# Projections of a two-layer decoder step: split single-pass products replaced by plain float32 products

## The chip, the cores and the metric

The kernel runs on one core of one Trainium2 chip. The metric is the device time of one execution in microseconds (us). TensorE is called PE in the profile and its weight loads PEld, VectorE DVE, ScalarE ACT, GpSimd POOL, and SyncE, which here orders nearly all transfers, SP (its queue SPq).

## The reference

One step of a decoder with two layers, all in float32: a retention layer, a shared key and value projection, and a block-sparse attention layer. 320 tokens pass through every projection: 256 of a prompt and 64 of eight sample sequences. The width is 1024.

```python
def retention_layer(x, pos, S0, chunk, norm_w, w_in, gn_w, w_out):
    h = rmsnorm(x, norm_w) @ w_in                  # 1024 -> q 1024 | k 1024 | v 2048 | gate 2048
    q, k, v, g = jnp.split(h, ...)
    q, k = rotary(q), rotary(k) * RET_DK ** -0.5
    S_fin, o = lax.scan(retention_chunk, S0, (q, k, v))
    y = (rmsnorm(o, gn_w) * silu(g)) @ w_out       # 2048 -> 1024
    return x + y, S_fin

def shared_kv(x, kv_norm_w, w_kv, k_norm_w):
    k, v = jnp.split(rmsnorm(x, kv_norm_w) @ w_kv, 2)   # 1024 -> 2048
    return rmsnorm(k, k_norm_w), v

def moba_query(x, norm_w, w_in, q_norm_w):
    q, g = jnp.split(rmsnorm(x, norm_w) @ w_in, 2)      # 1024 -> 2048
    ...
# attention over the own block and the past block, then * silu(g), @ moba_w_out (1024 -> 1024), + x
```

## The kernel before

The weights of all projections are cut into 52 chunks of 1 MB (`make_schedule`, `chunk_source`): `rq`, `rk`, `rv`, `rg` of each of four retention heads, `ro`, then `mq`, `mk`, `mv`, `mg`, `mo`. A chunk is loaded by SP into one of `RAW` = 3 slots of `w_raw`, two chunks ahead. One list of steps, written by hand in `make_schedule`, is walked by every engine, and each takes its own part of each step; a step `MM` is a piece of a projection (`project`), and the steps of the attention and retention work are put in the gaps between such pieces.

The projections are made with single-pass products (type fp32r). Each float32 operand is held as a rounded part and a remainder. For the weights, ACT writes the rounded part `w_hi` (`split_hi`, recorded at line 1246) and DVE the remainder `w_lo` (`split_lo`, line 1584), a quarter of a chunk at a time (steps `WS`), two chunks in turn. For the tokens they are `xn_hi`, `xn_lo` and `ym_hi`, `ym_lo`. A product is then three matmuls, hi·hi + hi·lo + lo·hi.

There are three kinds of step on PE, each for 128 rows of the inner dimension ("a k-step"):

- Line 944: 32 chunks (`rq`, `rk`, `rg`, `ro`, `mq`, `mg`), 128 weight columns as the stationary operand, 320 token columns moving. 32 chunks x 2 tiles x 8 = 512 k-steps, three matmuls each.
- Line 941: 20 paired chunks (`rv`, `mk`, `mv`, `mo`), 128 prompt tokens stationary, 512 weight columns moving. 20 x 2 tiles x 4 = 160 k-steps, three matmuls each.
- Line 925: the 64 sample tokens in the same 20 chunks. Their rounded parts and remainders stand side by side as 128 stationary columns (`stacked`), so a k-step is two matmuls, with `w_hi` and with `w_lo` moving: 80 k-steps. The upper 64 rows of the result are added to the lower ones afterwards (`lower_half`, `upper_half`).

Other products of the kernel that the prediction reads: the scores (line 1006), the states against the queries on four column tiles of 32 (line 1059), a sum over squares (line 1082) and the transposes (line 996); lines 1006, 1059 and 1082 are plain float32. In the program, a `matmul` of line 1082 stands once for each head, four in all.

Of the kernel before, what the change touches and what calls it, by code (L numbers as in the profile page):

```python
# [34 lines left out]
P = 128  # L35
D = 1024
# [12 lines left out]
RAW = 3  # L49
# [99 lines left out]
def make_schedule():  # L149
# [9 lines left out]
    def chunk(kind, a, b, gaps):  # L159
# [4 lines left out]
        starts = {0: 0} if n == 3 else {0: 0, 1: 2}  # L164
        mids = {0: 1, 1: 2, 2: 3} if n == 3 else {0: 1, 1: 3}
        size = KT // 2 if paired else KT
        whole = c + 1 if paired and b == 0 else c
        for pos, i in enumerate(tile_order(kind, a, b)):
            if pos in starts:
                steps.append(("WS", c + 1, starts[pos]))  # L170
# [10 lines left out]
            if pos in mids:  # L181
                steps.append(("WS", c + 1, mids[pos]))
# [131 lines left out]
def build(nc, a):  # L314
# [3 lines left out]
    with ctx:  # L318
# [113 lines left out]
        yf = flat_ktc[:, :, 2 * (TP + P):D]  # L432
# [11 lines left out]
        yfs = wide.ap().rearrange("p n k -> p (n k)")[:, 0:4 * P].rearrange("p (h i) -> p h i", h=MH)  # L444
# [22 lines left out]
        w_hi_done, w_lo_done, first_lo_done = sem("w_hi_done"), sem("w_lo_done"), sem("first_lo_done")  # L467
# [6 lines left out]
        unsplit_done = sem("unsplit_done")  # L474
        x_hi_done, x_lo_done = sem("x_hi_done"), sem("x_lo_done")
# [13 lines left out]
        y_done, y_hi_done, y_lo_done = sem("y_done"), sem("y_hi_done"), sem("y_lo_done")  # L489
# [21 lines left out]
        stack_done = sem("stack_done")  # L511
        q_done, gate_done, tanh_done = sem("q_done"), sem("gate_done"), sem("tanh_done")
        yf_done, yfs_done = sem("yf_done"), sem("yfs_done")
# [26 lines left out]

        def await_lo(eng, c, n):

            if c == 0 and n == 3:
                eng.wait_ge(first_lo_done, 1)
            else:
                eng.wait_ge(w_lo_done, 4 * c + n if c else (2, 1, 3)[n])
# [39 lines left out]
        hi_parts = [s for s in steps if s[0] in ("YA", "PG")]  # L586
        lo_parts = [s for s in steps if s[0] in ("YB", "PG")]

        def y_hi(*step):

            return 3 * KT + hi_parts.index(step) + 1

        def y_lo(*step):

            return 3 * KT + lo_parts.index(step) + 1

        def await_ret_over(eng):
# [4 lines left out]
            eng.wait_ge(y_lo_done, RH)  # L602
# [10 lines left out]
        def y_parts(h):  # L613

            k0 = 4 * (h % 2)
            hi, lo = (ym_hi, ym_lo) if h < 2 else (xn_hi, xn_lo)
            return hi[:, k0:k0 + 4, 0:T], lo[:, k0:k0 + 4, :]
# [50 lines left out]
        def _(sp):  # L668
# [197 lines left out]
        def _(pe):  # L866
# [18 lines left out]
            def project(step):  # L885
# [14 lines left out]
                hi, lo = chunk_view(w_hi, c, c % 2), chunk_view(w_lo, c, c % 2)  # L900
                x_hi, x_lo = xn_hi[:, :, 0:T], xn_lo
                if kind in ("mq", "mg") or (kind, h) == ("ro", 0):
                    x_hi, x_lo = ym_hi, ym_lo
                first = {"mq": 16, "mk": 24}.get(kind) if h == 0 and i == 0 else None
                stacked = paired and i == 2
                if stacked and h == 0 and k0 == 0:
                    pe.wait_ge(stack_done, {"rv": 1, "mk": 2, "mv": 2, "mo": 3 + part}[kind])
                for pos in range(k0, k1):
                    wk = FIRST_K[pos] if c == 0 else pos
                    k = base + wk  # L910
                    if c == 0:
# [3 lines left out]
                        pe.wait_ge(w_hi_done, pos // 2 + 1)  # L915
                        pe.wait_ge(x_hi_done, pos + 1)
                    elif i == tile_order(*chunks[c])[0] and paired:
                        await_lo(pe, c, wk)
                    elif i == 0 and not paired and k % 2 == 0:
                        await_lo(pe, c, k // 2)  # L920
                    if kind == "ro" and part == 0 and i == 0 and k % 4 == 0:
                        pe.wait_ge(y_lo_done, 2 * h + k // 4 + 1)
# [5 lines left out]
                    if first:  # L928
                        pe.wait_ge(x_lo_done, first - 8 + k + 1)
                    if kind == "mo" and h == 0 and i == 0:  # L930
                        pe.wait_ge(x_lo_done, y_lo("YB", k))
                    terms = ((hi, x_hi), (hi, x_lo), (lo, x_hi)) if c else ((hi, x_hi), (lo, x_hi), (hi, x_lo))
                    for n, (w, x) in enumerate(terms):
                        flags = {"start": base + pos == 0 and n == 0, "stop": k == KT - 1 and n == 2}
                        if c == 0 and n == 1:
                            await_lo(pe, c, k // 2)
                        elif c == 0 and n == 2:
                            pe.wait_ge(x_lo_done, pos + 1)
                        if paired:
                            c0, m = TOK[i]  # L940
                            mm = pe.matmul(bank[b][0:m, :], x[:, k, c0:c0 + m], w[:, wk, :], **flags)  # L941
                            continue
                        for tile, out in tiles:
                            mm = pe.matmul(bank[out][:, 0:T], w[:, wk, P * tile:P * tile + P], x[:, k, :], **flags)  # L944
                            if flags["stop"]:
                                close(mm, out)
# [281 lines left out]
        def _(act):  # L1228
# [6 lines left out]
            def split_hi(c, n):  # L1235

                if c >= nchunks:
                    return
                if c == 0 and n < 2:
                    act.wait_ge((second_w_loaded, first_w_loaded)[n], 16)  # L1240
                elif n == (2 if c == 0 else 0):
                    act.wait_ge(w_loaded[c % RAW], 16 * (c // RAW + 1))
                    if c >= 2:
                        await_chunk_used(act, c - 2)
                part = slice(CW // 4 * n, CW // 4 * (n + 1))
                act.activation(w_hi[:, c % 2, part], w_raw[:, c % RAW, part], ACT.Copy).then_inc(w_hi_done, 1)  # L1246

# [8 lines left out]
            for step in steps:  # L1256
                kind = step[0]
                if kind == "WS":
                    split_hi(*step[1:])
                elif kind == "XC" and step[2] == 1:  # L1260
                    await_full(act, 5, "UR", step[1])
                    act.activation(cross[:, :], bank[5][:, :], ACT.Copy).then_inc(bank_read[5], 1)
                elif kind == "W":
                    kt = step[1]
                    await_read(act, *tile_use("ro", KT + kt))
                    if kt == 0:
                        await_read(act, 3, "RP")
                        await_full(act, *tile_use("ro", KT - 1))
                    act.activation(ym_hi[:, kt, :], xT[:, kt, :], ACT.Copy, scale=wcols[:, W_MOBA + kt:W_MOBA + kt + 1])\
                        .then_inc(x_hi_done, 1)  # L1270
                elif kind == "SQ":
                    kt = step[1]
                    await_read(act, *tile_use("ro", KT + kt))
                    if kt == 0:
                        act.wait_ge(y_lo_done, RH)
# [5 lines left out]
                elif kind == "NB":  # L1281
                    kt = step[1]
                    if kt == KT:
                        continue
                    if kt == 0:
                        await_full(act, *tile_use("ro", 2 * KT - 1))
                    act.wait_ge(unsplit_done, kt + 1)
                    act.activation(xn_hi[:, kt, 0:T], scr[:, kt, :], ACT.Copy).then_inc(x_hi_done, 1)
                elif kind == "ST":
                    n = step[1]  # L1290
                    act.wait_ge(x_lo_done, (8, 24, y_lo("PG", 0), y_lo("PG", 1))[n])
                    if n:
                        await_full(act, *tile_use(*(("rv", 11), ("mv", 5), ("mv", 5))[n - 1]))
                    ks_at = slice(0, KT) if n < 2 else slice(4 * n - 8, 4 * n - 4)
                    if n == 0:
                        act.wait_ge(sums_done, 2)
                        act.activation(rms[:, 0:2], rms[:, 0:2], ACT.Sqrt, bias=eps[:, 0:1], scale=1.0 / D).then_inc(roots_done, 1)
                        act.activation(rms[0:TS, 2:3], rms[0:TS, 2:3], ACT.Sqrt, bias=eps[0:TS, 0:1], scale=1.0 / D)\
                            .then_inc(roots_done, 1)
# [805 lines left out]
```

## Time and profile before

| what | value |
|---|---|
| median of 3 runs | 501.36 us (498.37 to 502.27) |
| profiled execution | 499.55 us, its span 497.5 us |
| granted TensorE clock | 1.00 |
| PE busy | 490.3 us, 99% of the span |
| DVE, ACT, POOL busy | 353.1, 259.5, 95.9 us |
| transfers | 125.56 MB, mean 252 GB/s |

PE's busy time is the union of its instructions, whose ends are modelled: neighbours overlap, and the mean duration of one (317 ns) is longer than the distance from one start to the next. What a matmul occupies is read from the distance of the starts, or from the chain of work that ended last, where a run of matmuls is put down with its length and count.

### The profile page before, as it was taken

The numbers are of one execution on the slowest core, as the hardware profiler recorded it, in microseconds if no ns is written. First come the engines' busy times: TensorE is split into PE (matmuls) and PEld (weight loads), VectorE is DVE, ScalarE is ACT, GpSimd is POOL, SyncE is SP. The second block draws the span as 40 slices with busy tenths as digits, with TensorE's granted clock in tenths as the row PEclk, the third lists the DMA queues.
The fourth block names the chain that finished last, engine by engine and source line by source line (L and its number), as shares of the span: only waits on it lengthen the run. The fifth ranks groups of instructions, "written<-read, shape, count | busy, mean of one in ns | idle before, by whom it ended". The sixth has DMA issues, their size and how long they took to land.

```text
span 497.5 us, 9935 instructions
## 1 busy us (share of the span) xinstructions
PE 490.3 (99%) x3713; PEld 425.2 (85%) x3713; DVE 353.1 (71%) x629; ACT 259.5 (52%) x533; POOL 95.9 (19%) x139
## 2 busy tenths in 40 slices
PE   8999999999999999999999999999999999999997
PEld 7789978899778997799799999986777788999885
DVE  3875629895598838897189988897976764776631
ACT  5826533366416734385363454773747655555430
POOL 0192003620063200910000033437002000000000
PEclk9999999999999999999999999999999999999999
DMA  8984887999899998999946998999769666683211
GB/s 251 358 303 155 244 301 255 366 370 263 242 333 394 282 218 307 343 374 235 231 155 211 327 334 203 274 237 213 208 230 328 234 235 231 234 308 117 86 53 54
DMA packets 86915, 125.56 MB, mean 252 GB/s; under 512 B 5507, under 2 KB 51796, under 8 KB 86740
## 3 DMA queue, kind: packets, MB, share of 16 engines
q1 hardware_dynamic: 86018, 124.63, 80.8%
q8 instruction: 30, 0.49, 0.4%
q0 software_dynamic: 768, 0.28, 0.4%
q14 instruction: 17, 0.14, 0.1%
q10 hardware_dynamic: 82, 0.02, 0.0%
HBM read 98.93 MB, written 27.57 MB: 254 GB/s over the span
## 4 chain that ended last, share of the span: by engine, by line
PE 91%; DMA 3%; ACT 2%; DVE 1%; SPq 1%; issue 1%; DVEq 0%
PE bank L944 44%; PE bank L941 20%; PE bank L925 7%; DMA w_raw<-in_ret_w_in 3%; PE bank L1059 3%; PE bank L1121 2%; PE bank L1183 2%; PE bank L1073 1%; PE bank L1006 1%; PE bank L1222 1%; PE bank L1039 1%; PE bank L1041 1%; PE bank L1040 1%; PE bank L1027 1%; PE bank L1209 1%
## 5 line engine op out<-in xcount | busy, mean ns | idle before, releaser
L1584 DVE TENSOR_TENSOR w_lo<-w_raw,w_hi 128x512 fp32r<-128x512 f32 x207 | 145.2, 740 | 70.0 <-ACT w_hi L1246 69.3
L1246 ACT ACTIVATE w_hi<-w_raw 128x512 fp32r<-128x512 f32 x208 | 118.9, 620 | 70.2 <-PE bank L944 35.4
L944 PE MATMUL bank<-xn_hi,w_hi 128*128 128x320 f32 x320 | 100.0, 317 | 0.2 <-DVE raw_qk L1674 0.2
L944 PE MATMUL bank<-xn_hi,w_lo 128*128 128x320 f32 x320 | 97.7, 309 | 0.0
L944 PE MATMUL bank<-xn_lo,w_hi 128*128 128x320 f32 x320 | 97.5, 309 | 0.0
L941 PE MATMUL bank<-w_hi,xn_hi 128*128 128x512 f32 x160 | 65.1, 407 | 0.0
L944 PEld LDWEIGHTS bank<-xn_hi,w_hi 128*128 128x128 f32 x320 | 59.7, 188 | 3.9 <-issue 2.3
L941 PE MATMUL bank<-w_lo,xn_hi 128*128 128x512 f32 x160 | 62.6, 391 | 0.0
L941 PE MATMUL bank<-w_hi,xn_lo 128*128 128x512 f32 x160 | 62.4, 390 | 0.0
L944 PE MATMUL bank<-ym_hi,w_hi 128*128 128x320 f32 x192 | 60.9, 317 | 0.0
L944 PEld LDWEIGHTS bank<-xn_lo,w_hi 128*128 128x128 f32 x320 | 59.8, 188 | 0.3
L944 PEld LDWEIGHTS bank<-xn_hi,w_lo 128*128 128x128 f32 x320 | 59.7, 188 | 0.2 <-POOL w_lo L1985 0.2
L944 PE MATMUL bank<-ym_hi,w_lo 128*128 128x320 f32 x192 | 59.3, 309 | 0.0
L944 PE MATMUL bank<-ym_lo,w_hi 128*128 128x320 f32 x192 | 59.3, 309 | 0.0
L1798 DVE SCALAR_TENSOR_TENSOR st<-st,bank 128x512 f32<-128x512 f32 x64 | 39.6, 681 | 5.1 <-PE bank L1073 5.1
L944 PEld LDWEIGHTS bank<-ym_hi,w_hi 128*128 128x128 f32 x192 | 36.1, 188 | 1.8 <-issue 1.7
L2007 POOL TENSOR_TENSOR fin<-raw_qk,cst 128x320 f32<-128x320 f32 x16 | 16.9, 1076 | 106.1 <-DMA out_ret_state_prompt<-fin 96.8
L941 PEld LDWEIGHTS bank<-w_hi,xn_hi 128*128 128x128 f32 x160 | 30.0, 188 | 8.5 <-issue 3.1
L944 PEld LDWEIGHTS bank<-ym_lo,w_hi 128*128 128x128 f32 x192 | 36.1, 188 | 0.1
L944 PEld LDWEIGHTS bank<-ym_hi,w_lo 128*128 128x128 f32 x192 | 36.0, 188 | 0.0
L941 PEld LDWEIGHTS bank<-w_lo,xn_hi 128*128 128x128 f32 x160 | 30.0, 188 | 6.7
L941 PEld LDWEIGHTS bank<-w_hi,xn_lo 128*128 128x128 f32 x160 | 30.1, 188 | 5.5
(291 smaller groups left out, 777.1 us busy)
## 6 DMA issues: line engine op xcount, KB each, us to landing
w_raw<-in_ret_w_in SPq DMA_DIRECT2D x23, 1024.0 KB, 11.2
st<-in_state_ret SPq DMA_DIRECT2D x32, 512.0 KB, 8.7
out_ret_state_sample<-st SPq DMA_DIRECT2D x32, 512.0 KB, 3.8
w_raw<-in_ret_w_out SPq DMA_DIRECT2D x8, 1024.0 KB, 9.0
w_raw<-in_moba_w_in SPq DMA_DIRECT2D x8, 1024.0 KB, 6.3
w_raw<-in_w_kv SPq DMA_DIRECT2D x8, 1024.0 KB, 8.2
cache<-in_cache_v SPq DMA_DIRECT2D x16, 512.0 KB, 4.4
cache<-in_cache_k SPq DMA_DIRECT2D x44, 128.0 KB, 4.5
```

Of the source, the lines that this page charges most:

```text
L925: mm = pe.matmul(bank[b][:, :], xn_hi[:, k, TP:T + TS], w[:, wk, :], start=k == 0 and n == 0, stop=k == KT - 1 and n == 1)
L941: mm = pe.matmul(bank[b][0:m, :], x[:, k, c0:c0 + m], w[:, wk, :], **flags)
L944: mm = pe.matmul(bank[out][:, 0:T], w[:, wk, P * tile:P * tile + P], x[:, k, :], **flags)
L1006: mm = pe.matmul(bank[5][0:m, col:col + n], kT[:, d, j:j + m], qT[:, d, i0:i0 + n], start=d == 0, stop=d == 1)
L1027: mm = pe.matmul(o[:, P:TP], vp[:, 1, at], sT_own[:, :], start=False, stop=True)
L1059: mm = pe.matmul(bank[5][32 * j:32 * j + 32, :], qz[:, q0:q0 + 32], st[:, b, DV * d:DV * d + DV], start=False, stop=g == 1 and d == 1, ski ...
L1121: last[g] = pe.matmul(bank[PS_BANKS[g]][c0:c0 + 32, 0:PAST], wide[rows_at, 8 * h + 2 * e + q // 2, at:at + 32], turned(q, s)[rows_at, :, 4 ...
L1183: mm = pe.matmul(bank[7][32 * j:32 * j + 32, P * u:P * u + P], window(8 * half_at + 4 * (j // 2) + 2 * pg + j % 2, b % 4), page_at(16 + m) ...
L1246: act.activation(w_hi[:, c % 2, part], w_raw[:, c % RAW, part], ACT.Copy).then_inc(w_hi_done, 1)
L1584: dve.tensor_tensor(w_lo[:, c % 2, part], w_raw[:, c % RAW, part], w_hi[:, c % 2, part].bitcast(F32), ALU.subtract).then_inc(w_lo_done, 1)
L1798: dve.scalar_tensor_tensor(state, state, math.exp(NEW * LOG_DECAY[h]), bank[up_bank(b, d)][:, :], ALU.mult, ALU.add).then_inc(bank_read[up ...
L2007: done(pool.tensor_tensor(to, x, tab, ALU.mult))
```

## The change

All splitting of weights and tokens is gone. `w_raw` itself is the operand, the tokens are one tensor `xn` (and `ym`), and each k-step is one plain float32 matmul. `RAW` is 7, in the space that `w_hi` and `w_lo` took; SP orders two chunks ahead at first and up to six ahead later, and a slot is free when PE has used its chunk. For the sample tokens, 64 columns are stationary; even k-steps write rows 0 to 63 of the bank and odd ones rows 64 to 127, two column tiles of the array, and the halves are added as before.

```diff
-RAW = 3
+RAW = 7
...
-        w_hi = sb("w_hi", [P, 2, CW], F32R)
-        w_lo = sb("w_lo", [P, 2, CW], F32R)
...
-        xn_hi = sb("xn_hi", [P, KT, T + TS], F32R)
-
-        xn_lo = sb("xn_lo", [P, KT, T], F32R)
-        ym_hi = sb("ym_hi", [P, KT, T], F32R)
-        ym_lo = sb("ym_lo", [P, KT, T], F32R)
+        xn = sb("xn", [P, KT, T])
+        ym = sb("ym", [P, KT, T])
...
                 if c >= RAW:
-                    await_lo(sp, c - RAW, 2)
-                    await_lo(sp, c - RAW, 3)
+                    await_chunk_used(sp, c - RAW)
...
+            ordered = 2
             for step in steps:
                 kind = step[0]
                 if kind == "CHUNK":
                     c = step[1]
-                    load_chunk(c + 2)
+                    while ordered <= c + min(RAW - 1, 2 + c // 2):
+                        load_chunk(ordered)
+                        ordered += 1
...
+                if c and k0 == 0 and i == tile_order(*chunks[c])[0]:
+                    pe.wait_ge(w_loaded[c % RAW], 16 * (c // RAW + 1))
...
                     if stacked:
-                        for n, w in enumerate((hi, lo)):
-                            mm = pe.matmul(bank[b][:, :], xn_hi[:, k, TP:T + TS], w[:, wk, :],
-                                           start=k == 0 and n == 0, stop=k == KT - 1 and n == 1)
+                        rows_at = slice(TS * (k % 2), TS * (k % 2) + TS)
+                        mm = pe.matmul(bank[b][rows_at, :], x[:, k, TP:T], w[:, wk, :], start=k < 2, stop=k >= KT - 2,
+                                       skip_group_check=True)
                         continue
...
-                    terms = ((hi, x_hi), (hi, x_lo), (lo, x_hi)) if c else ((hi, x_hi), (lo, x_hi), (hi, x_lo))
-                    for n, (w, x) in enumerate(terms):
...
-                        for tile, out in tiles:
-                            mm = pe.matmul(bank[out][:, 0:T], w[:, wk, P * tile:P * tile + P], x[:, k, :], **flags)
...
+                    if paired:
+                        c0, m = TOK[i]
+                        mm = pe.matmul(bank[b][0:m, :], x[:, k, c0:c0 + m], w[:, wk, :], **flags)
+                        continue
+                    for tile, out in tiles:
+                        mm = pe.matmul(bank[out][:, 0:T], w[:, wk, P * tile:P * tile + P], x[:, k, :], **flags)
...
-                act.activation(w_hi[:, c % 2, part], w_raw[:, c % RAW, part], ACT.Copy).then_inc(w_hi_done, 1)
...
-                dve.tensor_tensor(w_lo[:, c % 2, part], w_raw[:, c % RAW, part], w_hi[:, c % 2, part].bitcast(F32),
-                                  ALU.subtract).then_inc(w_lo_done, 1)
```

The step lists of the two kernels place the same work in the same gaps. On PE, this is the end of a prompt tile and the start of the sample tile of chunk 8, the first `rv` chunk of the second head, in the kernel before (a name such as `bank<-w_hi,xn_lo` gives the output, the moving and the stationary operand):

```order
L941 MATMUL bank<-w_hi,xn_hi 128x512
L941 MATMUL bank<-w_hi,xn_lo 128x512
L941 MATMUL bank<-w_lo,xn_hi 128x512
L925 MATMUL bank<-w_hi,xn_hi 128x512
L925 MATMUL bank<-w_lo,xn_hi 128x512
```

and this the same place and the next chunk in the changed kernel, where L904 is a prompt k-step, L898 a sample k-step, L907 one with 320 token columns, and L1036, L1040 and L1045 are the old lines 1073, 1077 and 1082:

```order
L1036 MATMUL bank<-vq,kq 128x512 x4
L904 MATMUL bank<-w_raw,xn 128x512 x4
L898 MATMUL bank<-w_raw,xn 64x512 x4
L1040 MATMUL bank<-eye,scr 128x128 x4
L904 MATMUL bank<-w_raw,xn 128x512 x8
L898 MATMUL bank<-w_raw,xn 64x512 x2
L1045 MATMUL bank<-scr,ones 128x320
L898 MATMUL bank<-w_raw,xn 64x512 x2
L907 MATMUL bank<-xn,w_raw 128x320 x8
```

The three and the two matmuls of a k-step have become one, and the sample k-steps stand in 27 unbroken runs of two or four, which have another tile shape than nearly all of their neighbours.

On SP, the loads of chunks 2 to 6 before (L683 loads a chunk, L693 a state of a sample sequence):

```order
L683 DMA w_raw<-in_ret_w_in 128x4x512 x2
L683 DMA w_raw<-in_ret_w_in 128x8x256
L693 DMA st<-in_state_ret 128x2x512 x2
L683 DMA w_raw<-in_ret_w_in 128x8x256
L753 DMA bias_line<-gs 8x392
L754 DMA pages<-in_page_table 1x16
L756 DMA eye<-in_c_eye 128x4
L693 DMA st<-in_state_ret 128x2x512 x2
L683 DMA w_raw<-in_ret_w_in 128x8x256
L693 DMA st<-in_state_ret 128x2x512 x2
```

and now (L652 and L662 are the same two):

```order
L652 DMA w_raw<-in_ret_w_in 128x4x512 x2
L652 DMA w_raw<-in_ret_w_in 128x8x256 x2
L662 DMA st<-in_state_ret 128x2x512 x2
L652 DMA w_raw<-in_ret_w_in 128x8x256
L725 DMA bias_line<-gs 8x392
L726 DMA pages<-in_page_table 1x16
L728 DMA eye<-in_c_eye 128x4
L662 DMA st<-in_state_ret 128x2x512 x2
L652 DMA w_raw<-in_ret_w_in 128x8x256
L652 DMA w_raw<-in_ret_w_in 128x4x512
L662 DMA st<-in_state_ret 128x2x512 x2
```

One chunk more is ordered ahead of the first states, and two ahead of the third pair; before the last two, SP now waits until PE has used chunks 0 and 1.

On ACT, the start of the kernel before (L1297 and L1298 the roots for the norm, L1336 the copies of `xT`):

```order
L1246 ACTIVATE w_hi<-w_raw 128x512 x2
L1297 ACTIVATE rms<-rms,eps 128x2
L1298 ACTIVATE rms<-rms,eps 64x1
L1300 ACTIVATE xn_hi<-xn_lo 128x8x64
L1246 ACTIVATE w_hi<-w_raw 128x512 x4
L1336 ACTIVATE xT<-bank 128x320 x4
```

and now:

```order
L1263 ACTIVATE xn<-bank,wcols 128x320
L1287 ACTIVATE raw_qk,rms<-st 64x512
L1231 ACTIVATE rms<-rms,eps 128x2
L1232 ACTIVATE rms<-rms,eps 64x1
L1268 ACTIVATE xT<-bank 128x320 x4
L1327 ACTIVATE vp<-bank,rms 128x512 x2
```

The copies of `xT` no longer stand behind six weight splits, the last two of which waited for chunk 2.

## Rows read from the trace of the kernel before

**Rows 1.** The page: span, busy time of TensorE, and the chain by engine.

```profile
span 497.5 us, 9935 instructions
...
PE 490.3 (99%) x3713; PEld 425.2 (85%) x3713; DVE 353.1 (71%) x629; ACT 259.5 (52%) x533; POOL 95.9 (19%) x139
...
PE 91%; DMA 3%; ACT 2%; DVE 1%; SPq 1%; issue 1%; DVEq 0%
```

**Rows 2.** Waits of TensorE: who was waited for, us, times, longest.

```profile
PE bank L964 <- POOL eps L1964: 1.7, 1, 1.7
PE bank L1086 <- ACT xT L1336: 1.0, 1, 1.0
```

**Rows 3.** Groups of TensorE by form: count | busy us, mean ns of one.

```profile
L944 PE MATMUL bank<-xn_hi,w_hi 128*128 128x320 f32 x320 | 100.0, 317 | 0.2 <-DVE raw_qk L1674 0.2
...
L941 PE MATMUL bank<-w_hi,xn_hi 128*128 128x512 f32 x160 | 65.1, 407 | 0.0
...
L925 PE MATMUL bank<-w_hi,xn_hi 128*128 128x512 f32 x80 | 33.0, 413 | 0.0
...
L1059 PE MATMUL bank<-st,qz 128*32 128x512 f32 x128 | 14.6, 595 | 0.0
...
L1082 PE MATMUL bank<-scr,ones 128*128 128x320 f32 x8 | 2.8, 432 | 0.0
...
L996 PE MATMUL bank<-eye,kT 128*128 128x128 f32 x16 | 2.4, 271 | 0.0
```

**Rows 4.** The chain in order of time: start us, us, what.

```profile
33.39 1.81 PE bank L925 x8
35.20 5.44 PE bank L941 x24
...
42.45 3.52 PE bank L944 x24
...
71.68 3.57 PE bank L1059 x32
...
99.00 0.54 PE bank L1082 x2
...
103.98 0.44 PE bank L996 x4
```

**Rows 5.** Weight loads of TensorE (PEld), same columns as Rows 3.

```profile
L944 PEld LDWEIGHTS bank<-xn_hi,w_hi 128*128 128x128 f32 x320 | 59.7, 188 | 3.9 <-issue 2.3 <-DVE raw_qk L1674 0.7 <-DVE w_lo L1584 0.2
```

**Rows 6.** Timeline of TensorE, 51.35 to 52.3 us: start, us, what.

```profile
51.18 0.65 PE L1006 MATMUL bank<-qT,kT 128*128 128x128 f32 x5
51.76 0.42 PE L944 MATMUL bank<-xn_hi,w_hi 128*128 128x320 f32 x1
52.02 0.31 PE L944 MATMUL bank<-xn_lo,w_hi 128*128 128x320 f32 x1
```

**Rows 7.** Timeline of TensorE in the first two chunks.

```profile
22.11 0.31 PE L944 MATMUL bank<-xn_hi,w_lo 128*128 128x320 f32 x1
23.37 0.60 PE L1086 MATMUL bank<-fin 32*8 32x264 f32 x2 [0.95 <-ACT xT L1336]
24.14 0.41 PE L944 MATMUL bank<-xn_hi,w_hi 128*128 128x320 f32 x1 [0.17 <-DVE raw_qk L1674]
```

**Rows 8.** The chain before 24.14 us.

```profile
10.89 10.18 DMA w_raw<-in_ret_w_in
...
21.10 0.64 ACT w_hi L1246
...
21.76 0.56 DVE w_lo L1584
```

**Rows 9.** The page, transfers: KB each, us from issue to landing.

```profile
st<-in_state_ret SPq DMA_DIRECT2D x32, 512.0 KB, 8.7
```

**Rows 10.** Waits of the sync queue, same columns as Rows 2.

```profile
SPq L546 <- DVE w_lo L1584: 63.8, 12, 9.2
SPq L539 <- DVE st L1798: 62.1, 25, 13.0
```

More of the change, by code:

```diff
@@ L584, in x_pieces, with y_count @@
             return KT // 2 if chunks[c][0] in PAIRED else KT
[L586 to L595, printed above, removed]
+        gated = [s for s in steps if s[0] in ("YA", "PG")]
+        def y_count(*step):
+            return 3 * KT + gated.index(step) + 1
         def await_ret_over(eng):
@@ L899, in project @@
                     await_free(pe, b, "TILE", whole, i)
[L900 to L903, printed above, removed]
+                w = chunk_view(w_raw, c, c % RAW)
+                x = ym if kind in ("mq", "mg") or (kind, h) == ("ro", 0) else xn
+                if c and k0 == 0 and i == tile_order(*chunks[c])[0]:
+                    pe.wait_ge(w_loaded[c % RAW], 16 * (c // RAW + 1))
                 first = {"mq": 16, "mk": 24}.get(kind) if h == 0 and i == 0 else None
                 stacked = paired and i == 2
-                if stacked and h == 0 and k0 == 0:
-                    pe.wait_ge(stack_done, {"rv": 1, "mk": 2, "mv": 2, "mo": 3 + part}[kind])
+                if stacked and kind == "mo" and h == 0 and k0 == 0:
+                    pe.wait_ge(x_done, y_count("PG", part))
                 for pos in range(k0, k1):
@@ L914, in project @@
                             turn_x(2, *TOK[2], range(4, KT))
[L915 to L920, printed above, removed]
-                    if kind == "ro" and part == 0 and i == 0 and k % 4 == 0:
-                        pe.wait_ge(y_lo_done, 2 * h + k // 4 + 1)
+                        if pos % 2 == 0 and pos < 6:
+                            pe.wait_ge((first_w_loaded, second_w_loaded, w_loaded[0])[pos // 2], 16)
@@ L923, in project @@
+                        pe.wait_ge(x_done, pos + 1)
+                    if kind == "ro" and part == 0 and i == 0 and k % 4 == 0:
+                        pe.wait_ge(y_moved, 2 * h + k // 4 + 1)
+                    if first:
+                        pe.wait_ge(x_done, first - 8 + k + 1)
+                    if kind == "mo" and h == 0 and i == 0:
+                        pe.wait_ge(x_done, y_count("YA", k))
                     if stacked:
-                        for n, w in enumerate((hi, lo)):
-                            mm = pe.matmul(bank[b][:, :], xn_hi[:, k, TP:T + TS], w[:, wk, :],
-                                           start=k == 0 and n == 0, stop=k == KT - 1 and n == 1)
+                        rows_at = slice(TS * (k % 2), TS * (k % 2) + TS)
+                        mm = pe.matmul(bank[b][rows_at, :], x[:, k, TP:T], w[:, wk, :], start=k < 2, stop=k >= KT - 2,
+                                       skip_group_check=True)
@@ new lines, in project @@
+                    flags = {"start": base + pos == 0, "stop": k == KT - 1}
+                    if paired:
[4 more added lines that the diff above has]
+                        mm = pe.matmul(bank[out][:, 0:T], w[:, wk, P * tile:P * tile + P], x[:, k, :], **flags)
+                        if flags["stop"]:
+                            close(mm, out)
@@ L1257, in _ @@
                 kind = step[0]
-                if kind == "WS":
-                    split_hi(*step[1:])
-                elif kind == "XC" and step[2] == 1:
+                if kind == "XC" and step[2] == 1:
                     await_full(act, 5, "UR", step[1])
@@ L1280, in _ @@
                         .then_inc(bank_read[5], 1)
[L1281 to L1299, printed above, removed]
-                    act.activation(xn_hi[:, ks_at, T:T + TS], xn_lo[:, ks_at, TP:T].bitcast(F32), ACT.Copy).then_inc(stack_done, 1)
+                elif kind == "ST" and step[1] == 0:
+                    act.wait_ge(sums_done, 2)
+                    act.activation(rms[:, 0:2], rms[:, 0:2], ACT.Sqrt, bias=eps[:, 0:1], scale=1.0 / D).then_inc(roots_done, 1)
+                    act.activation(rms[0:TS, 2:3], rms[0:TS, 2:3], ACT.Sqrt, bias=eps[0:TS, 0:1], scale=1.0 / D)\
+                        .then_inc(roots_done, 1)
                 elif kind == "RP":
@@ L1344, in _ @@
                     scaled(0)
-                    split_hi(0, 0)
                     scaled(1)
@@ L1494, in _ @@
                         await_full(act, *tile_use("rg", 15))
-                    act.activation(y_parts(h)[0], y_now(h), ACT.Copy).then_inc(y_hi_done, 1)
+                    act.activation(y_at(h), y_now(h), ACT.Copy).then_inc(y_moved, 1)
                 elif kind == "MB":
@@ L1625, in _ @@
                 kind = step[0]
[L1626 to L1634 removed]
+                if kind == "NORM":
                     for kt in range(2):
@@ L1683, in _ @@
                     done.wait()
-                elif kind == "NB":
+                elif kind == "NB" and step[1] < KT:
                     kt = step[1]
-                    if kt < KT:
-                        normed(kt, W_KV, xT[:, kt, :])
-                    if kt:
-                        dve.wait_ge(x_hi_done, 2 * KT + kt)
-                        dve.tensor_tensor(xn_lo[:, kt - 1, :], scr[:, kt - 1, :], xn_hi[:, kt - 1, 0:T].bitcast(F32),
-                                          ALU.subtract).then_inc(x_lo_done, 1)
+                    if kt == 0:
+                        await_full(dve, *tile_use("ro", 2 * KT - 1))
+                    dve.scalar_tensor_tensor(xn[:, kt, :], xT[:, kt, :], wcols[:, W_KV + kt:W_KV + kt + 1], rsb[:, :],
+                                             ALU.mult, ALU.mult).then_inc(x_done, 1)
                 elif kind == "MP":
@@ L1845, in _ @@
                         own_values_lo(step[1] + 1)
-                elif kind == "SH":
-                    h = step[1]
-                    dve.wait_ge(y_hi_done, h + 1)
-                    hi, lo = y_parts(h)
-                    dve.tensor_tensor(lo, y_now(h), hi.bitcast(F32), ALU.subtract)\
-                        .then_inc(y_lo_done, 1)
                 elif kind == "MB":
@@ L1968, in _ @@
             cos, sin = cst[:, C_COS:C_COS + T], cst[:, C_SIN:C_SIN + T]
-            part = slice(3 * CW // 4, CW)
             def spread_queries(h):
```

142 lines of the change are left out of this document (19 added, 123 removed).

## The prediction

> **What bounds the kernel now.** I read the page first, then the waits of TensorE, its groups by form, and the chain in order of time. The page has PE busy for 99% of the span, and 91% of the chain that ended last is PE's own work [rows 1]. The view has six waits of PE, and only two reach a microsecond: 1.7 us before anything is loaded, and 1.0 us in the second chunk [rows 2]. So no wait on the splits of ACT and DVE bounds this kernel, however busy these two are; the matmuls themselves do. What the change is worth is decided by one question: does a k-step take PE longer as one plain float32 product than as three (or two) single-pass ones?
>
> The mean durations of the groups (317 ns, 432 ns) are not what a matmul occupies, since neighbours overlap. The chain gives the distances [rows 4]. 24 single-pass matmuls of 320 columns take 3.52 us, 0.147 each; 24 of 512 columns take 5.44 us, 0.227 each; 8 of line 925 take 1.81 us, 0.226 each.
>
> **The projections before.** 512 k-steps x 3 x 0.147 = 225.8 us; 160 x 3 x 0.227 = 109.0; 80 x 2 x 0.226 = 36.2. Together 371 us of a span of 497.5.
>
> **A plain product of 320 columns.** Line 1082 is this very shape, in plain float32. It stands four times in the program and has 8 records [rows 3], so a plain product is recorded as two, and the two occupy 0.54 us of the chain [rows 4]. That is 0.27 for a record against 0.147 for a single-pass product of equal width: each record streams the columns twice. A weight load takes 188 ns [rows 5] and fits under a record of 270. A k-step goes from 0.441 to 0.54 us: 512 x 0.10 = **+51 us** (the bounds 0.535 and 0.55, the rounding of the row and some margin, give +48 to +56).
>
> **A plain product of 512 columns.** By width, 0.54 x 512 / 320 = 0.864 us. The states against the queries (line 1059) have 512 columns too, on four column tiles: 32 records in 3.57 us are eight rounds of 0.446, the entry into this shape included, or 0.89 for two rounds [rows 4]. I take 0.86, since the row includes an entry of about 0.1. The k-step was 0.681: 160 x 0.18 = **+29 us** (+28 to +33).
>
> **The sample tokens.** One product of 64 stationary columns costs its full stream, 0.86 us, but even and odd k-steps stand on different column tiles. Line 1059 shows that column tiles run beside each other: 32 records, each of 0.43 us by width, would take 13.8 us one after another and take 3.57 [rows 4]. With two tiles I take full overlap, 0.43 us for a k-step, against 0.45 before: 80 x -0.02 = **-2 us**. With no overlap at all it would be 80 x 0.41 = +33; nothing in the row reads that way.
>
> **Changing the tile shape.** These k-steps were of full width and are now 27 runs of half width between full ones. What such a change costs is seen where line 1006 goes to 64 columns and back [rows 6]. One record of 128 columns and four of 64 start at 51.18; by 0.54/640 us for a column they occupy 0.32 us, so PE would be free at 51.50, and the next matmul starts at 51.76: 0.26 us for in and out. The one after it comes 0.26 later instead of 0.147, another 0.11, because its weight load could not be made ahead; behind a record of 0.27 us it would nearly hide. 27 x 0.26 = 7.0, with a part of the 0.11 some **+8 us** (from +4, if runs next to other shapes change nothing, to +10).
>
> The Trainium skill has a rule that speaks against the change at this place: changing the tiling mode, not just the tile, drains TensorE (TensorEngine Tiling, "Key Properties"). The trace agrees with it in kind, by the 0.26 us just read, and the page gives no figure, so the sum would be the same.
>
> **What the change gives back on PE.** In the order of the program I count 86 runs of projection matmuls that follow other work. Each now loses about 0.11 us at its second matmul [rows 6], since a weight load of 188 ns is longer than a product of 147 and could not be made ahead. Behind records of 0.27 and 0.43 us it mostly hides: 86 x 0.06 = **-5 us** (0 to -9).
>
> **The start.** PE waits 0.95 us at 23.37 for ACT's copies of `xT`, in a gap of 1.26 us between starts, and once more before 24.14 [rows 7]. Behind it stand the splits of chunk 2: its load lands at 21.07, ACT splits until 21.74, DVE goes on [rows 8]. Without splits the copies of `xT` come earlier and these gaps go, **-1.7 us** (0 to -2.5). Later is then only PE itself, whose first two chunks grow by their k-steps.
>
> **What costs nothing.** The splits on ACT and DVE, four on each for each of 52 chunks, leave engines that PE almost never waits for. Where tokens are scaled, one instruction replaces two or three; no wait of PE ends there now [rows 2]. The seven slots hide loads that are hidden already: no wait of PE for a weight load is among its waits from the second chunk on. If that cover went, a load would have to come a whole chunk late, and six ahead makes it less likely.
>
> **The new wait on SP.** A slot is now free when PE has used a chunk, so at every chunk SP stands until the chunk before it is used, where it stood for the last split, 63.8 us in all [rows 10]. Behind it are queued the loads and stores of the sample states, the key pages, and the rows through memory for the next update; PE's line 1059 waits for those states. SP already keeps pace with the state updates, 62.1 us of waits for DVE's `st` [rows 10], which are in the same chunks as PE. I take 0, and a bound below.
>
> **Sum.** 51 + 29 - 2 + 8 - 5 - 1.7 = +79.3 us. The profiled execution took 499.55 us, which gives 579; the median of the runs is 1.8 above it. I predict **580 us**, a ratio of 1.157. The terms' own bounds, taken together (low ends +69, high ends +95), would make 570 to 596; not all err on one side, so I hold 572 to 590 for this case.
>
> **Rivals.**
>
> *Two column tiles overlap only in part.* A plain product is two records. If records start strictly in program order, then the two of one product stand back to back on their own tile, and only the second of one product runs beside the first of the next: four k-steps take five slots of 0.43 us instead of four, two k-steps three instead of two. That is one slot more for each run, 27 x 0.43 = +11.6: **592 us**. Against it: by the same rule the 32 records of line 1059 would be paired at best and take 6.9 us, and they take 3.57 [rows 4]. The Trainium skill says that matmuls start and end in program order and are never reordered (TensorE: Matmul & The Clock Gate, Part 3, "The mechanism"); the row of line 1059 does not go with it for products of two records, unless the build interleaves them. Chance 0.08.
>
> *No overlap of the two tiles:* +35 on the sum, **615 us**. Against it, the same row. Chance 0.03.
>
> *SP comes late.* If in each of the three heads with states to reload the last states land one landing time too late (8.7 us [rows 9]), PE stands 26 us: **606 us**. It decides once SP reaches a load later than 8.7 us before its product; a chunk will take PE 8.6 us, so the margin is about a chunk. Against it: states are loaded a whole head ahead of use. Chance 0.05.
>
> *Not slower: the projections as one record.* The transposes on line 996 are float32 too and have 16 records for 16 in the program, four in 0.44 us, a single pass [rows 3, 4]. Were the plain projections also one record, a k-step would cost 0.27, 0.43 and 0.22 us: 138 + 69 + 17 = 224 us instead of 371, and the kernel would take about **353 us**. The change breaks even where a plain k-step of 320 columns costs about 0.45 us. Against it stands line 1082, a plain product and no transpose, with two records and 0.54 us. Chance 0.015.
>
> **How the numbers follow.** The forecast's mechanism has 0.82, at 580 us. With the first rival (592) included and margins for a term that I did not see, the range is 570 to 596. Within 1% of the time before, which is about what a measurement of this kernel can tell from no change, lies none of the cases: chance 0.005; faster 0.015; slower 0.98.
>
> **What the profile will show.** Line 907 with 1024 records at 0.27 us distance, line 904 with 320 at 0.43, line 898 with 160 records, those of a run in some 0.9 us for two k-steps and 1.7 for four. In the chain, a run of eight 320-column k-steps at 4.3 us where 24 matmuls took 3.52. PE still at 99%, DVE and ACT under half. The gap before 24.14 gone. Wrong would be: sample runs of four at 2.1 us (first rival) or 3.4 (second); waits of PE for `st`, `cache` or `vq` (third); and if PE's records stand at these distances and the time is still under 570, then PE was not the bound that I took it for.

## The result, and the profile after

The changed kernel takes 580.79 us (median of 4 runs, 580.18 to 581.63) against 499.87 for the kernel before, a ratio of 1.162 with a 95% interval of 1.156 to 1.168. The forecast was 580 us. The profiled execution took 580.18 us. The change is worth +80.9 us by the medians and +80.8 by the two spans (578.3 against 497.5); +79.3 was forecast. The kernel before was 1.5 us faster in this comparison than in the one that the forecast started from (501.36), so the time came out nearer to its forecast than the difference did.

The page after, to be read against [rows 1]:

```profile
span 578.3 us, 7987 instructions
...
PE 572.9 (99%) x3041; PEld 341.1 (59%) x3041; DVE 195.1 (34%) x384; ACT 142.8 (25%) x303; POOL 75.6 (13%) x138
...
PEclk9999999999999999999999999999999999999999
...
PE 98%; DMA 1%; SPq 0%; issue 0%; DVE 0%; DVEq 0%
PE bank L907 48%; PE bank L904 24%; PE bank L898 7%; PE bank L1022 2%; PE bank L1084 2%; PE bank L1146 1%; PE bank L1036 1%; PE bank L969 1%; DMA st<-in_x_prompt 1%; PE bank L1185 1%; PE bank L1003 1%; PE bank L1002 1%; PE bank L1004 1%; PE bank L1172 1%; PE bank L990 1%; PE bank L1179 1%
```

PE is busy for 99% of the span as before, and now 98% of the chain is its own work. DVE fell from 353 to 195 us of busy time and ACT from 260 to 143, and nothing came of it, as the waits of PE before foretold. The waits of PE after, the answer to [rows 2]:

```profile
PE bank L927 <- POOL eps L1821: 1.7, 1, 1.7
PE bank L1084 <- issue: 0.4, 1, 0.4
```

The wait for ACT's `xT` in the second chunk is gone; the first row is the same wait at the very start. The groups by form, the answer to [rows 3] (L907 is the old 944, L904 the old 941, L898 the old 925):

```profile
L907 PE MATMUL bank<-xn,w_raw 128*128 128x320 f32 x640 | 179.8, 436 | 0.0
L904 PE MATMUL bank<-w_raw,xn 128*128 128x512 f32 x320 | 145.6, 599 | 0.0
L907 PE MATMUL bank<-ym,w_raw 128*128 128x320 f32 x384 | 106.9, 433 | 0.0
L898 PE MATMUL bank<-w_raw,xn 128*64 128x512 f32 x160 | 40.3, 609 | 0.0
```

1024, 320 and 160 records: each of the 512, 160 and 80 plain products is recorded as two, as line 1082 was. The chain over the first `rv` chunks gives their lengths, the answer to [rows 4]:

```profile
28.42 6.87 PE bank L904 x16
35.29 1.87 PE bank L898 x8
37.16 7.06 PE bank L904 x16
...
51.25 4.31 PE bank L907 x16
```

Eight k-steps of 320 columns (16 records) take 4.31 us, 0.539 each, against 0.441. Eight of 512 take 6.87 us, 0.859 each, against 0.680. Four sample k-steps (8 records) take 1.87 us where four before took 1.81: two tiles do run beside each other, or it would be 3.4. The next run of eight, right behind the sample tokens, takes 7.06 us and not 6.87; that is the way out of the narrow shape.

The start, the answer to [rows 7]: between the two parts of the second chunk the product of line 1049 (the old 1086) now follows at once.

```profile
20.96 2.42 PE L907 MATMUL bank<-xn,w_raw 128*128 128x320 f32 x8
23.31 0.61 PE L1049 MATMUL bank<-fin 32*8 32x264 f32 x2
23.85 2.42 PE L907 MATMUL bank<-xn,w_raw 128*128 128x320 f32 x8
```

PE is at 23.85 us where it was at 24.14 before, with longer k-steps behind it.

### The profile page after: what moved, and what is told of

It is laid out like the page before. It is cut to its first block, busy times and chain, and to the rows that moved or that the text cites. A ratio compares the mean times of both kernels' runs of the same rounds, so it can differ in the third digit from the quotient of the medians.

```text
span 578.3 us, 7987 instructions
## 1 busy us (share of the span) xinstructions
PE 572.9 (99%) x3041; PEld 341.1 (59%) x3041; DVE 195.1 (34%) x384; ACT 142.8 (25%) x303; POOL 75.6 (13%) x138
## 4 chain that ended last, share of the span: by engine, by line
PE 98%; DMA 1%; SPq 0%; issue 0%; DVE 0%; DVEq 0%
PE bank L907 48%; PE bank L904 24%; PE bank L898 7%; PE bank L1022 2%; PE bank L1084 2%; PE bank L1146 1%; PE bank L1036 1%; PE bank L969 1%; DMA st<-in_x_prompt 1%; PE bank L1185 1%; PE bank L1003 1%; PE bank L1002 1%; PE bank L1004 1%; PE bank L1172 1%; PE bank L990 1%; PE bank L1179 1%
## 5 line engine op out<-in xcount | busy, mean ns | idle before, releaser
L907 PE MATMUL bank<-xn,w_raw 128*128 128x320 f32 x640 | 179.8, 436 | 0.0
L907 PEld LDWEIGHTS bank<-xn,w_raw 128*128 128x128 f32 x640 | 119.2, 190 | 52.1 <-issue 5.9
L904 PE MATMUL bank<-w_raw,xn 128*128 128x512 f32 x320 | 145.6, 599 | 0.0
L907 PE MATMUL bank<-ym,w_raw 128*128 128x320 f32 x384 | 106.9, 433 | 0.0
L904 PEld LDWEIGHTS bank<-w_raw,xn 128*128 128x128 f32 x320 | 57.9, 190 | 70.2 <-issue 69.8
L907 PEld LDWEIGHTS bank<-ym,w_raw 128*128 128x128 f32 x384 | 71.7, 190 | 29.5 <-issue 1.7
L898 PE MATMUL bank<-w_raw,xn 128*64 128x512 f32 x160 | 40.3, 609 | 0.0
L898 PEld LDWEIGHTS bank<-w_raw,xn 128*64 128x64 f32 x160 | 9.1, 135 | 20.1 <-issue 19.4
L1022 PE MATMUL bank<-st,qz 128*32 128x512 f32 x128 | 14.6, 595 | 0.0
L1860 POOL TENSOR_TENSOR raw_qk<-raw_qk,cst 128x320 f32<-128x320 f32 x16 | 13.5, 863 | 0.6
```

The costliest lines, as they stand in the source:

```text
L898: mm = pe.matmul(bank[b][rows_at, :], x[:, k, TP:T], w[:, wk, :], start=k < 2, stop=k >= KT - 2, skip_group_check=True)
L1022: mm = pe.matmul(bank[5][32 * j:32 * j + 32, :], qz[:, q0:q0 + 32], st[:, b, DV * d:DV * d + DV], start=False, stop=g == 1 and d == 1, ski ...
L1860: done(pool.tensor_tensor(to, x, tab, ALU.mult))
```

## The experiments

They ask four things: whether the form of the products is the whole difference, what each term of the sum measures, whether the order of the loads matters, and where PE would stop being the bound.

### e1 and e9: the products of before, without any split

```diff
-                        mm = pe.matmul(bank[b][0:m, :], x[:, k, c0:c0 + m], w[:, wk, :], **flags)
+                        for t in range(3):
+                            mm = pe.matmul(bank[b][0:m, :], x[:, k, c0:c0 + m], wr[:, wk, :],
+                                           start=flags["start"] and t == 0, stop=flags["stop"] and t == 2)
```

Here `wr` is one rounded chunk, type fp32r like `xn`, which stands in for all chunks; the 320-column k-steps are edited in the same way, and the sample k-steps are two products of 128 stationary columns. e9 also orders loads two ahead (`while ordered <= c + 2`).

> The changed kernel, but every k-step again in the form of the kernel before: three single-pass products for prompt and 320-column k-steps, two of full width for the sample tokens. No splits: all three products of a k-step are the same one, of rounded tokens and of rounded weights of the first chunk, which stand in for all chunks (all loads and waits for them stay). It leaves out the remainders and the weights of 51 chunks, so its values are not the reference's. Theory (PE's products are the time, the splits were hidden): the time of the kernel before less the stall in its second chunk, 498 us (496 to 500). Rival (the splits on ACT and DVE held PE back beyond its visible waits): under 490.

e1 measured 503.26 us (12 runs), ratio to the kernel before 1.006 (1.002 to 1.009). It was neither of the two. The waits of PE in it:

```profile
PE bank L1089 <- issue: 3.2, 1, 3.2
PE bank L932 <- POOL eps L1836: 1.7, 1, 1.7
PE bank L1103 <- DVE ps L1758: 1.4, 1, 1.4
```

The first and the third row are 4.6 us. The first is in the scores against the cached keys, and in the chain there stands one transfer of a key page:

```profile
344.92 9.24 DMA cache<-in_cache_k
```

The median landing of such a page was 4.5 us in the kernel before. The waits cost more than their own length. Behind them PE's products take longer:

```profile
368.49 3.71 PE bank L899 x8
372.20 3.22 PE bank L906 x12
```

In the 5 us from 365 to 370 us the mean granted clock is 0.62, so most of them pass at the lower of its two levels (1.2 GHz), and from 370 to 380 it is 0.85. The one long landing gave a new theory, that six weight loads in the queues delay the pages.

> e1_form_before with the weight loads two chunks ahead throughout, still in seven slots. e1 came out at 503.3 us, 5 above what its products alone give: PE waits 3.2 us in one place, in the scores against the cached keys, for a key page that took 9.2 us to land behind weight loads. Theory (the six-ahead order puts weight loads in front of the pages in the transfer queues): that wait goes and the time is that of the kernel before or 1.5 us less, 498 to 500. Rival (the wait comes of SP's later place in its list, or of chance): 503 again.

e9 measured 497.13 us (12 runs), ratio to the kernel before 0.996 (0.992 to 0.9995), and a little under what was expected, and both waits are gone:

```profile
PE bank L932 <- POOL eps L1836: 1.7, 1, 1.7
PE bank L848 <- DMA st<-in_x_sample: 0.3, 1, 0.3
```

The same two runs of products are back at their lengths:

```profile
362.30 2.04 PE bank L899 x8
364.34 2.72 PE bank L906 x12
```

Between 345 and 378 us of e1's trace PE loses 8.0 us against the same work in e9's: 4.7 are the waits, and most of the other 3.3 is the lower clock behind them.

So the form of the products is the whole difference: with 158 us less of busy time on DVE and 115 on ACT (353.1 to 194.5, 259.5 to 144.7), the time is 1.9 us from that of before. (e7 below is the changed kernel with the same order of loads.) And the six-ahead order is not free as soon as PE is fast enough to reach a page early; it costs 5 us by the ratios of e1 and e9 and 6 by their medians. The theory may be only a part of the reason. The median landing of a page is 6.8 us in e1 and 4.9 in e9, so the pages do land later. But SP also orders them later: it stood 13.6 us for a free slot in e1 and never for one in this stretch of e9, and it ordered the page of the long landing at 344.9 us, where the same page was ordered at 335.8 in e9. No run separates the two.

### e7: two ahead in the changed kernel

> The changed kernel with loads two chunks ahead throughout, in seven slots. Theory (loads were and are hidden): 581 us, within 0.3%. Rival (the six-ahead order is what keeps PE from waiting): PE's waits name w_raw, and the time rises by several us. Rival (six ahead delays the states): faster.

580.72 us (7 runs), ratio to the kernel before 1.162 (1.157 to 1.167): the same as six ahead. In the slower kernel the order of loads is neither gain nor loss. PE's wait at the cached keys was there in its profile too:

```profile
PE bank L1084 <- issue: 2.2, 1, 2.2
```

The profiled execution is the longest of the seven (583.92 us) and one of two with a granted clock below 1.00, so the 2.2 us are not what a usual execution has. Whether they, against 0.4 in the changed kernel, are the order or chance is open.

### e2 and e3: one kind of k-step after the other

e2 leaves the sample k-steps as in the change, e3 also the prompt k-steps of 512 columns; the rest are three single-pass products as in e1.

> As the previous kernel, with the sample tokens alone as in the change: plain float32 on two column tiles. Theory: -2 us for overlapping tiles and +10 for 27 entries and exits of the shape (0.36 us each by the trace of the changed kernel), so 8 above the previous one, 506 us. Rival 1 (changes of shape cost nothing of their own): 496. Rival 2 (the tiles overlap only in part): 518 or more.

509.29 us (4 runs), 6.0 above e1. Expected were 8. Both have the waits for pages, 4.6 us in e1 and 3.7 in e2, and a stretch of low clock behind them, which is shorter in e2. Without either, e2's span of 506.2 us is some 501 (worked out below), and that is 7 above e9's 493.9.

> As the previous kernel, with the 160 prompt k-steps of 512 columns plain too; only the 320-column k-steps are three single-pass products, of rounded operands and the first chunk's weights. Theory: 160 x 0.18 = +28 us, 534 us, and the rest to the changed kernel, +46, is the 320-column k-steps. Rival (the cost of plain products lies in going over from one kind to the other, not in their columns): the mix would be as slow as the changed kernel or slower, 570 or more.

529.97 us, one run. PE's waits at the pages are gone here, as PE is slower, so e2 is to be taken without its 3.7 us of waits and without the 1.6 us that the low clock behind them cost (eight sample matmuls take 3.13 us there and not 1.87, the twelve single-pass ones behind them 3.34 and not 3.0). By the spans, 528.1 less 500.9, the plain 512-column k-steps cost 27 us; by the distances in the chain it is 160 x 0.179 = 28.6. From e3 to the changed kernel it is +50.8 us, the 320-column k-steps, against 512 x (0.539 - 0.441) = 50.2 by the chain. The mix of both kinds runs at the lengths of each alone (960 + 576 matmuls of line 909 with a mean of 312 ns as before, 320 records of line 905 as in the changed kernel):

```profile
L909 PE MATMUL bank<-xn,w_one 128*128 128x320 f32 x960 | 148.9, 312 | 0.0
L905 PE MATMUL bank<-w_raw,xn 128*128 128x512 f32 x320 | 145.6, 599 | 0.0
```

So no cost shows that hangs on going over from one kind to the other.

### e5 and e6: the two column tiles

```diff
-                        rows_at = slice(TS * (k % 2), TS * (k % 2) + TS)
+                        rows_at = slice(TS * (k // 7), TS * (k // 7) + TS)
...
-                        mm = pe.matmul(bank[b][rows_at, :], x[:, k, TP:T], w[:, wk, :], start=k < 2, stop=k >= KT - 2,
+                        mm = pe.matmul(bank[b][rows_at, :], x[:, k, TP:T], w[:, wk, :], start=k in (0, 7), stop=k >= KT - 2,
```

> The changed kernel with seven of the eight sample k-steps of a tile on the lower column tile and the eighth on the upper: same products, same shape, same number of shape changes, hardly any overlap. Theory (two column tiles run beside each other in full): 7 slots of 0.86 us instead of 4 for each of ten sample tiles, +26 us, 607 us. Rival (the two tiles never overlapped): same, 581. Rival (half overlap): +13.

605.25 us, one run: +24.5 on the changed kernel, close to the 26 of full overlap. In its chain four sample k-steps take 3.58 us, which is the length without overlap and with the shape change kept:

```profile
34.96 3.58 PE bank L898 x8
38.54 7.07 PE bank L904 x16
```

```diff
-                        mm = pe.matmul(bank[b][rows_at, :], x[:, k, TP:T], w[:, wk, :], start=k < 2, stop=k >= KT - 2,
-                                       skip_group_check=True)
+                        mm = pe.matmul(bank[b][:, :], x[:, k, TP - TS:T], w[:, wk, :], start=k == 0, stop=k == KT - 1)
```

> The changed kernel with 128 stationary columns in the sample k-steps, plain float32, no column tiles: the last 64 prompt tokens stand beside the 64 sample tokens, so that their product is added in and the values are not the reference's. Theory: +80 x 0.43 = +34.4 us for the lost overlap, and -9.7 for 27 entries and exits at 0.36 us that go: 605.5 us. Rival (shape changes cost nothing): 615.

606.06 us (4 runs), +25.3 on the changed kernel. In its chain four sample k-steps take 3.43 us and the run behind them is back at 6.87:

```profile
35.47 3.43 PE bank L897 x8
38.90 6.87 PE bank L902 x16
```

Against the changed kernel's 1.87 and 7.06 and e5's 3.58 and 7.07 this gives the price of the shape: 0.15 us on the way in (3.58 - 3.43) and 0.20 on the way out (7.07 - 6.87), 0.35 for a run, 9.4 us for 27. Then 34.3 us of overlap lost less 9.4 is 24.9, and 25.3 were measured. Both rivals on overlap are out: 1.87 less 0.15 is 1.72, four slots of 0.43 and not five. The Trainium skill's rule that matmuls start and end in program order (TensorE: Matmul & The Clock Gate, Part 3, "The mechanism") does not go with this for products of two records, unless the build interleaves them, which no run here shows.

### e10: the stall at the start of the kernel before

```diff
-            if pos in starts:
+            if pos in starts and not (c == 1 and pos == 0):
                 steps.append(("WS", c + 1, starts[pos]))
```

The two `WS` steps now stand behind `RP`, the step that copies `xT`.

> The kernel before, with the step that copies xT and prepares the norm factors placed ahead of the first half of chunk 2's weight splits on ACT and DVE. Theory (PE's gap of 1.26 us at 22.11 and part of the 0.2 before 24.14 come of that order): 1.0 to 1.7 us less, ratio 0.997, perhaps not to be told from the kernel before by its time, but by the gap in the profile. Rival (the splits of chunk 2 come too late instead): PE waits for w_lo at 28 us.

498.78 us (12 runs) against 499.01, ratio 0.9989 (0.9951 to 1.0028): not to be told from no change. The gap itself is gone,

```profile
21.65 0.31 PE L948 MATMUL bank<-xn_hi,w_lo 128*128 128x320 f32 x1
21.89 0.61 PE L1090 MATMUL bank<-fin 32*8 32x264 f32 x2
22.43 0.41 PE L948 MATMUL bank<-xn_hi,w_hi 128*128 128x320 f32 x1
```

PE goes on with the second chunk at 22.43 us and not at 24.14, and the span is 496.0 instead of 497.5. The -1.7 of the prediction is shown as a gap, not as a time.

### e8, e4 and e11: fewer products, until PE is not the bound

> The kernel of three single-pass products without splits, cut to two for each k-step (two for the sample tokens as before); it leaves out a third product and the remainders. Theory: PE's work falls by 512 x 0.147 + 160 x 0.227 = 111.6 us, 387 us; the transfers need 321 at the rate of the busiest slices and stay hidden for the most part. Rival (transfers or attention already set the time): over 400, with PE's waits naming them.

449.93 us, one run, 63 above the forecast. Its page and the longest waits of PE:

```profile
span 448.0 us, 7996 instructions
...
PEclk9999979999859999799999996998888999999999
```

```profile
PE bank L1041 <- issue: 16.1, 2, 11.0
PE bank L1089 <- DVE mvp L1748: 8.1, 1, 8.1
PE bank L1027 <- DMA st<-in_state_ret: 5.4, 3, 4.4
```

Line 1041 (the old 1073) is the update of the states. "issue" is time in which PE waited for nothing that the profile shows; the chain before it is the new values written to memory and read back:

```profile
101.48 7.49 DMA v_rows<-vs_split
...
110.31 10.98 DMA vq<-v_rows
```

This landing ends at 121.3 us and PE's wait at 126.9, so it covers half of the 11.0; for the last 5.6 us no cause is shown. All waits of PE add up to 47.5 us. The granted clock, nearly always at its full level of 2.4 GHz in the kernels above, falls around the places where PE waited; its mean is 0.946. That is the likely rest of the 63 us, though it was not measured by itself.

> As the first kernel of this call, with one single-pass product for each k-step; it leaves out two thirds of the products. PE would need 371 / 3 = 124 us for the projections (sample k-steps 18 of them) and 108 for the rest, some 236 in all. Theory: PE is the bound only as long as it has more work than the transfers; at the 391 GB/s of the busiest slices 125 MB need 321 us, so 330 to 380 us with PE waiting for loads. Rival (PE alone sets the time at every size): about 245. Rival (the attention work on ACT and DVE takes over): PE's waits name them and not the loads.

430.9 us, one run, again above all I had expected, with the mean clock at 0.821:

```profile
span 429.0 us, 6492 instructions
...
PEclk9679959869955989559699695886667869999699
```

```profile
PE bank L1041 <- issue: 17.9, 2, 9.9
PE bank L1089 <- DVE mvp L1748: 14.4, 2, 8.8
PE bank L1027 <- DMA st<-in_state_ret: 14.0, 2, 10.8
```

Cutting the third product saved 53 us against e1, cutting the second only 19 more. What took over is not the rate of the transfers, which stayed at 280 and 292 GB/s in the mean. It is waits at one place after another, and the clock that PE loses by them: 122.5 us of waits in e4. Of these 19.1 name a transfer, 17.9 stand as "issue", and 85.5 name another engine, among them 13.3 for ACT's `ym` and 10.6 for DVE's `gs`, which are no transfers. So the rival of the attention and retention work on ACT and DVE holds for a part; how much of the rest lies behind transfers in the end was not traced.

> e8_two_products with loads two chunks ahead. e8 took 450 us, not the 387 of its products: PE waited 16 us for vq (rows written to memory and read back, 7.5 and 11 us of landing), 8 for transposes of key pages, 5 for states. Theory (six-ahead weight loads lengthen these landings): the waits shrink and the time falls to 400 to 430. Rival (the landings are long because all transfers together are at their rate, whatever their order): 445 to 455 again.

440.7 us, one run, 9 below e8, and between the two expectations. The main wait is still there, and one for weights is new:

```profile
PE bank L1041 <- issue: 14.6, 2, 8.9
PE bank L911 <- DMA w_raw<-in_ret_w_out: 4.7, 1, 4.7
PE bank L1089 <- DVE mvp L1748: 4.6, 1, 4.6
```

There the same two landings take 7.9 and 10.0 us. So six ahead is not what makes the way through memory long; my theory for e8 falls. Whether the 9 us are the order or chance, one run each doesn't tell. What the landings consist of stays open. During them e8 moves 355 and 211 GB/s and e11 363 and 232, so the second landing is long at a low rate; the transfer engines are busy all through it (their share is 1.09 and 1.08), and no run here separates what keeps them busy.

## Why the prediction was right

- **PE's matmuls are the bound.** Shown by e9: the same products without the splits take the same time within 0.4%.
- **A plain product of 320 columns, 0.54 us, +51.** 0.539 in the chain, +50.2; +50.8 from e3 (one run) to the changed kernel.
- **A plain product of 512 columns, 0.86 us, +29.** 0.859 in the chain, +28.6; +27 by the spans of e2 and e3, with the waits and the low clock of e2 taken off.
- **Sample tokens, full overlap, -2.** 0.43 us for a k-step, -1.9; shown by e5 and e6.
- **The tile shape, +8.** 0.35 us for each of 27 runs, +9.4. It was mis-sized by little: I had taken the weight load behind the way out to be nearly hidden; it is not. The Trainium skill says that a change of the tiling mode drains TensorE (TensorEngine Tiling, "Key Properties"), without a figure; the runs agree, by 0.35 us a run.
- **Run starts, -5: this term does not hold.** It took the second matmul of a run to be late and to catch up behind longer records. It does: over the 72 runs of lines 944 and 941 that follow other work, the second matmul is late by 6.5 us in sum before and by 3.3 after, by the starts in the traces. But the first matmul of these runs now starts later behind the last matmul of the other work, 15.6 us in sum where it was 12.7. Both together, less a normal distance for each run, are 19.3 us in the kernel before, 19.0 in e9 and 18.9 in the changed kernel: nothing is given back. The reading looked at one side of the border only. Why the first matmul is later is open.
- **The start, -1.7.** The gap went in the changed kernel and in e10 by that much.
- **The sum.** The terms measured add up to 50.2 + 28.6 - 1.9 + 9.4 - 1.7 = +84.6, and the difference of the medians is +80.9. Of the -3.7 left over, a part is rounding: over all its runs line 941 has 0.2286 us from start to start and not 0.227, which makes the 512-column term +27.6, and the shape by the spans of e6 (34.3 - 25.2) is +9.1. Some 2 us are not placed.
- **The seven slots cost and gain nothing:** right here (e7). What I did not see is that the order of loads costs 5 to 6 us in a kernel with the faster products (e1 against e9).
- **SP's new wait, 0.** SP stands longer for slots than it stood for the splits, and no wait of PE ends in it:

```profile
SPq L652 <- PE bank L907: 106.3, 15, 15.2
SPq L652 <- PE bank L898: 54.9, 10, 10.2
SPq L829 <- ACT rows L1303: 44.9, 3, 39.4
SPq L522 <- DVE st L1667: 43.4, 20, 12.3
```

- **The rival of one record for a product** is out by the counts of records.

The mechanism of the forecast, PE as the bound and the two plain lengths read from rows, is what the runs show. That the number came so near is in part luck. The other terms were forecast at +84.3 and measure +83 to +85, which alone would make 583 to 584 for the profiled execution, where 580.2 was measured; the -5 stands for something that gives nothing back, and happens to cover the 2 to 4 us that no term explains. The bounds of the prediction were also added up wrongly: its terms' low ends make +66.5 and its high ends +97, not +69 and +95, which would be 568 to 598. The result lies far inside either.

## What to carry to other kernels

Count passes, not instructions. At 2.4 GHz the 0.539 us of a plain product of 320 columns are 1294 cycles, or 4.0 for a column, and the 0.147 us of a single-pass one are 1.1. So one plain float32 product costs as much as four passes over its columns, and the split form has three; the splits that looked wasteful on two other engines were free, and their removal could only pay if PE had been waiting for them. The trace of before held the price of the new form in a line that stood four times in the program; look for such a row before anything else. A gain that is read from the distance behind the first matmul of a run has to be read before it as well. And where an operand narrows, its overlap with a neighbour has to be weighed against what every entry and exit of the narrow shape costs.

## What was not expected of the hardware

- A change from 128 to 64 stationary columns and back costs 0.35 us of PE: 0.15 in, 0.20 out. Half of the way out is the second record of the next product: behind a sample run it starts 0.533 us after the first and not 0.429.
- Two records of one plain product do not keep two column tiles from overlapping in full: 8 records of 0.43 us in 1.72 us.
- A single-pass product of fp32r takes 0.147 us for 320 columns and 0.227 for 512, a quarter of a plain one 0.135 and 0.215: some 12 ns more each. It is 1536 x 12 ns, or 18 us, of the kernel before, for line 944 alone.
- A wait of PE costs more than its length, as the granted clock falls around it. In e1 two waits of 1.4 and 3.2 us within 11 us were followed by a stretch at the lower level that cost another 3 us. With PE busy for 89% of the span (e8) the mean granted clock was 0.946, and with 71% (e4) it was 0.821, against 1.00 in the kernel before and in the changed one.
